# Expert items of 32 rows in four column groups of TensorE, sums kept in four PSUM banks, a ring of ten weight slots, and an opening in halves

## The reference

```python
def first_block(x, attn_norm, w_in, ...):
    for l in range(DEPTH):                      # 2 layers
        h = rms_norm(x, attn_norm[l])
        proj = h @ w_in[l]                      # the first products of the kernel
        ...                                     # retention, sparse attention, gating, FFN
def moe_ffn(h, router_w, router_b, w_gu, b_gu, w_down, b_down):
    logits = (xt @ router_w + router_b).astype(f32)
    top_val, top_idx = lax.top_k(logits, TOP_K) # 4 of 32 experts for each token
    gate = jax.nn.softmax(top_val, axis=-1)
    ...                                         # tokens grouped by expert
    gu = xblk @ w_gu[e] + b_gu[e]               # 1024 -> 2048
    g, up = gu[:, :D_FF_2], gu[:, D_FF_2:]
    g = jnp.minimum(g, SWIGLU_LIMIT)
    up = jnp.clip(up, -SWIGLU_LIMIT, SWIGLU_LIMIT)
    act = (up + 1.0) * (g * jax.nn.sigmoid(SWIGLU_ALPHA * g))
    act @ w_down[e] + b_down[e]                 # 1024 -> 1024, times the gate, summed per token
h = h + g2 * rmsnorm(ff, ffn_post_g)            # ff: the sum over the token's experts
```

## Time and profile before

| | us |
|---|---|
| median of three runs | 1902.48 (1902.21 to 1903.59) |
| the profiled execution | 1903.54 |
| its span, first to last instruction | 1901.6 |
| PE busy | 1843.2 (97%) |
| PE busy in gate-up, L2087 (x2000) | 440.0 |
| PE busy in down, L2110 (x912) | 203.2 |
| DVE busy | 771.0 (41%) |
| DVE L1405, additions to the accumulator (x136) | 93.5 |
| longest wait of SP: for PE L2087, 80 times | 291.2 in total |

### The profile page before, as it was taken

The page is one execution under the profiler, slowest core; times in us unless marked ns, Lnnn a source line. Parts: engine busy times, 40 slices in busy tenths (PEclk is TensorE's granted clock), DMA queues, the critical chain, the costliest instruction groups (busy, mean ns, idle before and its releaser), DMA issues.

```text
span 1901.6 us, 22803 instructions
## 1 busy us (share of the span) xinstructions
PE 1843.2 (97%) x8198; PEld 920.0 (48%) x8199; DVE 771.0 (41%) x1594; ACT 231.2 (12%) x466; POOL 207.5 (11%) x398
## 2 busy tenths in 40 slices
PE   8999999999999999999899999999999999999997
PEld 4466777754667777675433333333333333333332
DVE  3553111135635774288542333233233233323334
ACT  1321000004211000223100100010010001000101
POOL 0200000002004867512000000000000000000000
PEclk9999999999999999999999999999999999999999
DMA  8143344342338884406699999999999499999995
GB/s 317 67 148 126 132 178 165 123 168 89 127 145 342 316 329 172 160 26 242 236 416 429 427 428 429 428 428 429 429 427 427 203 429 429 429 428 428 429 428 231
DMA packets 41016, 558.01 MB, mean 293 GB/s; under 512 B 4567, under 2 KB 5463, under 8 KB 6525
## 3 DMA queue, kind: packets, MB, share of 16 engines
q1 hardware_dynamic: 40380, 556.13, 70.9%
q10 hardware_dynamic: 576, 1.11, 0.2%
HBM read 556.16 MB, written 1.06 MB: 293 GB/s over the span
## 4 chain that ended last, share of the span: by engine, by line
PE 77%; DMA 13%; DVE 8%; issue 1%; ACT 1%; ACTq 0%; DVEq 0%; SPq 0%; POOLq 0%
PE PS L2087 19%; PE PS L1776 16%; DMA mega<-in_exp_w 12%; PE PS L2110 10%; PE PS L1504 8%; PE PS L1795 8%; PE PS L1681 3%; PE PS L1972 1%; PE PS L2069 1%; PE PS L1818 1%; PE PS L2076 1%; PE PS L1812 1%; DVE K L1421 1%; DVE tb L1422 1%; DVE tmp L1418 1%; DVE tb L1419 1%
## 5 line engine op out<-in xcount | busy, mean ns | idle before, releaser
L2087 PE MATMUL PS<-mega,tb 128*64 128x512 f32 x2000 | 440.0, 594 | 6.2 <-POOLq L2234 6.2
L1776 PE MATMUL PS<-hT,mega 128*128 128x256 f32 x1376 | 300.6, 379 | 0.0
L2087 PEld LDWEIGHTS PS<-mega,tb 128*64 128x64 f32 x2000 | 139.8, 137 | 300.5 <-issue 281.8
L1776 PEld LDWEIGHTS PS<-hT,mega 128*128 128x128 f32 x1376 | 261.1, 190 | 43.0 <-issue 8.6
L2110 PE MATMUL PS<-mega,tb 128*64 128x512 f32 x912 | 203.2, 596 | 3.7
L1504 PE MATMUL PS<-mega,hT 128*128 128x512 f32 (+2 forms) x448 | 187.9, 561 | 3.1 <-ACT hT L448 3.1
L1418 DVE TENSOR_SCALAR tmp<-PS 128x512 f32<-128x512 f32 x34 | 23.5, 692 | 368.9 <-PE PS L2087 368.9
L1795 PE MATMUL PS<-mega,late 128*128 128x512 f32 x352 | 154.7, 593 | 0.0
L1109 DVE TENSOR_TENSOR late<-PS,late 128x512 f32<-128x512 f32 x22 | 15.2, 692 | 270.3 <-PE PS L1776 270.3
L2110 PEld LDWEIGHTS PS<-mega,tb 128*64 128x64 f32 x912 | 64.6, 137 | 120.4 <-issue 118.8
L1504 PEld LDWEIGHTS PS<-mega,hT 128*128 128x128 f32 x448 | 81.7, 192 | 72.2 <-issue 60.0
(11 more groups left out here) (459 smaller groups left out, 1687.5 us busy)
## 6 DMA issues: line engine op xcount, KB each, us to landing
mega<-in_exp_w SPq DMA_DIRECT2D x171, 2048.0 KB, 23.4
mega<-in_w_gate_up SPq DMA_DIRECT2D x22, 2048.0 KB, 8.1
late<-in_exp_w SPq DMA_DIRECT2D x21, 2048.0 KB, 25.4
mega<-in_ada_w SPq DMA_DIRECT2D x12, 2048.0 KB, 9.3
mega<-in_w_in_part SPq DMA_DIRECT2D x10, 2048.0 KB, 9.7
mega<-in_w_down SPq DMA_DIRECT2D x10, 2048.0 KB, 7.3
mega<-in_w_out SPq DMA_DIRECT2D x6, 2048.0 KB, 8.4
mega<-in_w_in SPq DMA_DIRECT2D x4, 2048.0 KB, 8.2
```

What stands on the lines that cost most here:

```text
L1776: ins = pe.matmul(PS[:, 4 + 2 * (i % 2) + part, 256 * f:256 * f + 256], wt[:, k, 256 * part + 128 * f:256 * part + 128 * f + 128], hT[:, k ...
L2087: ins = pe.matmul(PS[64 * h:64 * h + 64, b, :], xg[:, o:o + 64], slot_of(r, s)[:, w:w + 512], start=False, stop=k == KC - 1, skip_group_ch ...
```

## The change

It alters five things.

1. An item holds 32 rows. The reference's counts then give 49 items: 17 experts have one, 13 have two (experts 0, 6, 9, 10, 11, 16, 20, 22, 23, 24, 28, 29, 31), two have three (17 and 18). Gate-up has 4 products of 32 rows by 512 columns a step, in four column groups side by side; down has 4 of 32 rows by 256 columns a step. Gate and up of an item now lie side by side in one bank, so all of DVE's and ACT's operations on an item are 256 columns wide and not 512. Transposes are 2 for each of the activations, the scatter weights and the next rows.
2. The scatter adds into four PSUM banks (4 to 7) over all items, 8 products of 32 by 256 an item; the additions in SBUF are gone. The scatter is one piece, after the gather. The down result, the turned scatter weights and the bias get other banks, and the bias product of the next item stands ahead of down.
3. The ring has ten slots (a new tile, `tenth`), and the PE loop is written for five experts in place of three. A load takes the place of the one ten loads earlier; slot 3 of expert 1 is loaded right after expert 0's six.
4. The end: no additions; ACT's squares read PSUM in four operations of 512, DVE multiplies by the gain out of PSUM.
5. The opening: `x` and the first block come in two halves each, the constants' first part (with the gains) on ACT's queue, the big constants table later; TensorE runs products on zeros while it waits, turns the first half of `x`, does four products of the first block, then turns the second half.

```diff
-SLOTS, SLOT_TURNS = 9, 3
+SLOTS, SLOT_TURNS = 10, 5
@@ SP, opening
-            sp.dma_start(ident, a["constants"][:, 0:K_FLIP]).then_inc(g.s_id, 16)
-            sp.dma_start(x[:], a["x"][0].rearrange("(t p) d -> p t d", p=P)).then_inc(g.s_x, 16)
+            sp.dma_start(x[:, 0, :], a["x"][0, 0:P, :]).then_inc(g.s_id, 16)
...
                 if n == 0:
-                    sp.dma_start(K[:, K_FLIP:K_ALL], a["constants"][:, K_FLIP:K_ALL]).then_inc(g.s_k, 16)
+                    sp.dma_start(ring[:, slot, 0:width // 2], src[:, 0:width // 2]).then_inc(g.r_ssm, 16)
+                    sp.dma_start(x[:, 1, :], a["x"][0, P:2 * P, :]).then_inc(g.s_x, 16)
+                    sp.dma_start(ring[:, slot, width // 2:width], src[:, width // 2:width]).then_inc(landed[slot], 16)
+                    continue
@@ SP, experts
+            sp.wait_ge(landed[3], 16 * LOADS_BEFORE[3] + 16)
+            sp.dma_start(slot_of(1, 3), a["exp_w"][1, 3]).then_inc(landed[3], 16)
...
-                for s in range(3 if e == 1 else 0, RING):
-                    last = (s + 3) % RING
-                    sp.wait_ge(freed[last], (before if s < 3 else done) + (USES_BEFORE[last] + 1))
+                for s in range(4 if e == 1 else 0, RING):
+                    last = (s + 2) % RING
+                    sp.wait_ge(freed[last], (before if s < 4 else done) + (USES_BEFORE[last] + 1))
@@ DVE, one item
-                ch.to(v.tensor_scalar(mgs, PS[:, 0, :], SWIGLU_LIMIT, None, ALU.min), g.m_gs, n + 1)
-                ch(v.tensor_scalar(mus, PS[:, 1, :], SWIGLU_LIMIT, -SWIGLU_LIMIT, ALU.min, ALU.max))
+                ch.to(v.tensor_scalar(mgs, PS[:, 0, 0:256], SWIGLU_LIMIT, None, ALU.min), g.m_gs, n + 1)
+                ch(v.tensor_scalar(mus, PS[:, 0, 256:512], SWIGLU_LIMIT, -SWIGLU_LIMIT, ALU.min, ALU.max))
+                expert_row(ch, after, n + 2)
...
-                add_half(ch, 0, 2 * n + 2)
...
+                ch.to(v.tensor_copy(pwT, PS[:, 1, 256:512]), g.m_pwe, n + 2)
+                modulated(ch, n + 2)
                 scatter_rows(ch, after, n + 2)
@@ PE, opening
+            pe.wait_ge(g.s_tab, 2)
+            zero_products(512, 384)
+            pe.wait_ge(g.s_id, 32)
...
+                    pe.wait_ge(g.r_ssm, 16)
+                    pe.wait_ge(g.s_hd, 1)
+                    part(0, range(4))
+                    pe.wait_ge(g.s_x, 16)
+                    turn_x(1, g.s_xt)
...
+                    part(0, range(4, KC)).then_inc(g.s_pj, 1)
...
+                    part(1, range(KC)).then_inc(g.s_pj, 1)
@@ PE, one item
-                        for b in range(2):
-                            for h in range(2):
-                                w = 2048 * kk + 1024 * b + 512 * h
-                                ins = pe.matmul(PS[64 * h:64 * h + 64, b, :], xg[:, o:o + 64], slot_of(r, s)[:, w:w + 512],
-                                                start=False, stop=k == KC - 1, skip_group_check=True)
+                        for j in range(4):
+                            w = 2048 * kk + 512 * j
+                            ins = pe.matmul(PS[32 * j:32 * j + 32, 0, :], xg[:, o:o + ITEM], slot_of(r, s)[:, w:w + 512],
+                                            start=False, stop=k == KC - 1, skip_group_check=True)
                     ins.then_inc(freed[s], 1)
                 gather(n + 2)
...
+                scatter(n + 1)
...
+                bias_rows(n + 2)
                 pe.wait_ge(g.m_ate, n + 1)
+                pe.wait_ge(g.m_pwe, n + 2)
                 for c in range(KC):
...
-                    for h in range(2):
-                        o = 1024 * (c % 4) + 512 * h
-                        ins = pe.matmul(PS[64 * h:64 * h + 64, 2, :], aT[:, P * (c % 4) + 64 * (c // 4):P * (c % 4) + 64 * (c // 4) + 64],
-                                        slot_of(r, s)[:, o:o + 512], start=c == 0, stop=c == KC - 1, skip_group_check=True)
+                    o = P * (c % 2) + ITEM * (c // 2)
+                    for j in range(4):
+                        w = 1024 * (c % 4) + 256 * j
+                        ins = pe.matmul(PS[32 * j:32 * j + 32, 1, 0:256], aT[:, o:o + ITEM], slot_of(r, s)[:, w:w + 256],
+                                        start=c == 0, stop=c == KC - 1, skip_group_check=True)
```

More of the change, by code:

```diff
@@ L333, in slot_of @@
             at = (6 * r + s) % SLOTS
-            return late[:, 0:4096] if at == SLOTS - 1 else mega[:, 4096 * at:4096 * at + 4096]
-        oacc = hTf.rearrange("p (t n) -> p t n", t=TT)
+            if at >= 8:
+                return late[:, 0:4096] if at == 8 else tenth[:]
+            return mega[:, 4096 * at:4096 * at + 4096]
+        normed = hTf.rearrange("p (t n) -> p t n", t=TT)
         tmp2 = tmp[:, 0:1024]
@@ L914, in _ @@
                     link.to(v.tensor_tensor(brow, PS[0:NH, 2, :], oh[0:NH, 512:1024], ALU.add), g.s_b0, 1)
+                else:
+                    v.wait_ge(g.s_par, 16 * l + 16)
+                    for t in range(TT):
+                        v.wait_ge(g.s_xt, TT * l + t + 1)
+                        turned(g.s_hd, TT * l, t, par[:, PC_ATTN:PC_ATTN + 8])
+                        row_squares(t)
                 rsqrt(mean_eps(2, D), 2, dst=y_in)
                 v.sem_inc(g.s_y, 1)
-                if l == 0:
-                    v.wait_ge(g.s_k, 16)
                 projected(0)
@@ L1374, in _ @@
             ends, owner = tmp[:, 0:32], tmp[:, 64:64 + MAX_ITEMS]
-            link(v.tensor_scalar(ends, PS[:, 0, 64:96], 64.5, None, ALU.is_gt))
-            for lim_ in (128.5, 192.5):
-                link(v.scalar_tensor_tensor(ends, PS[:, 0, 64:96], lim_, ends, ALU.is_gt, ALU.add))
+            whole = tmp[:, 128:160].bitcast(I32)
+            link(v.tensor_scalar(ends, PS[:, 0, 64:96], -1.0, 0.0, ALU.add, ALU.max))
+            link(v.tensor_copy(whole, ends))
+            link(v.tensor_scalar(whole, whole, 5, None, ALU.logical_shift_right))
+            link(v.tensor_copy(ends, whole))
             link(v.tensor_tensor_scan(tmp[:, 32:64], K[:, K_ONE:K_ONE + 32], ends, 0.0, ALU.mult, ALU.add))
@@ L2042, in turn_gathered @@
                 pe.wait_ge(g.m_xr, value)
-                for c in range(4):
-                    ins = pe.transpose(PS[:, 3, P * c:P * c + P], xr[:, P * c:P * c + P], ident)
+                for c in range(2):
+                    ins = pe.transpose(PS[:, 3, 256 + P * c:256 + P * c + P], xr[:, P * c:P * c + P], ident)
                 ins.then_inc(g.m_xt, 1)
@@ L2055, in _, with summed @@
             pe.wait_ge(g.act2, ACT2["m_gc"] + 1)
-            for b, bank in enumerate((2, 4, 6, 7)):
-                rows_b = slice(32 * b, 32 * b + 32)
-                ins = pe.matmul(PS[:, bank, :], gT[rows_b, P * (b // 2):P * (b // 2) + P], p2[rows_b, Q_BD + 512 * (b % 2):Q_BD + 512 * (b % 2) + 512],
-                                start=True, stop=True)
+            def summed(t, j):
+                return PS[:, 4 + j, 256 * t:256 * t + 256]
+            for t in range(TT):
+                for j in range(4):
+                    rows = slice(32 * j, 32 * j + 32)
+                    ins = pe.matmul(summed(t, j), gT[rows, P * t:P * t + P], p2[rows, Q_BD + 256 * j:Q_BD + 256 * j + 256],
+                                    start=t == 0, stop=False, skip_group_check=True)
             ins.then_inc(g.pe2, 1)
@@ L2063, in _, with bias_rows @@
             items = pe.value_load(item_i[0:1, ENDS_AT + 31:ENDS_AT + 32], min_val=N_EXPERTS, max_val=MAX_ITEMS)
[L2065 to L2069 removed]
+            def bias_rows(value):
+                pe.wait_ge(g.m_es, value)
+                pe.matmul(PS[:, 0, :], esel, bgu, start=True, stop=False, skip_group_check=True)
+            def scatter(value):
+                pe.wait_ge(g.m_pwe, value)
+                pe.wait_ge(g.m_ye, value)
+                for t in range(TT):
+                    for j in range(4):
+                        rows = slice(32 * j, 32 * j + 32)
+                        ins = pe.matmul(summed(t, j), pwT[rows, P * t:P * t + P], ysb[rows, :], start=False, stop=False, skip_group_check=True)
                 ins.then_inc(g.m_s, 1)
             def item(n, r):
[L2073 to L2076 removed]
                 pe.wait_ge(g.m_xge, n + 1)
@@ L2128, in _ @@
                     item(n, r)
-            pe.wait_ge(g.m_ye, items + 1)
-            pe.wait_ge(g.m_pwe, items + 1)
-            for t in range(TT):
-                for h in range(2):
-                    rows = slice(64 * h, 64 * h + 64)
-                    ins = pe.matmul(PS[:, 3 * t + h, :], pwT[rows, P * t:P * t + P], ysb[rows, :], start=True, stop=True)
-                ins.then_inc(g.m_s, 1)
+            scatter(items + 1)
         @block.gpsimd
```

218 lines of the change are left out of this document (116 added, 102 removed).

## The result

The changed kernel takes 1908.6 us, the median of nine runs (1907.5 to 1910.4), beside 1902.5 for the kernel before on the same chip, also nine runs (1901.7 to 1903.9). The ratio is 1.0032, with a 95% interval of 1.0022 to 1.0042. So it is slower, by 6.1 us, where 4.0 us faster was forecast. Its profiled execution has a span of 1905.9 us, where 1897.6 was worked out.

A forecast was written before the change was run, and what follows sets the result against it. Transfers were to become the bound: last slot at 1872.0, remaining work to 1903.2, less 7.5 for the opening, plus 0.9 and 1.0: span 1897.6, median 1898.5 us. Likeliest case (0.60) 1891 to 1905; with rivals 1885 to 1912.

The forecast's parts named there:

- The item: Expert loop: gate-up 6.84, 3.34 until down, down 3.43 us; 13.6 an item, 13.7 with a gap.
- it just fits: Between gate-up and down: TensorE's own work of 3.4 us fits beside the chain of 3.3.
- P': Time from one item to the next in the changed kernel: 13.7 us, said to count seven times in the end.
- The stream's start: Weight transfers resume at 967.0 on the earlier profile's axis; tenth slot wins 4.9 us, expert 0's second item costs 11.0.
- 182 loads: Weight loads still to go once the stream resumes, at 4.90 us each.
- Experts 17 and 18: Stream stands 1.5 and 11.7 us around these experts of three items, 13.2 in place of 25.4.
- The end: After the last slot at 1872.0: 2.2, 1.7 and a whole item, then a tail of 13.6 us, to 1903.2.
- The opening: Kernel start: first product at 7.4, first block's work done at 34.3, 7.5 us earlier, carried through to the end.
- two additions: Added to 1895.7: 0.9 us for reading the next expert's loop bounds, 1.0 for half clock behind waits.
- Groups that overlap less: Rival, column groups: with three of four overlapping P' is 17.1 and time 1922; today's pairs, over 1965; chance 0.13.
- The clock: Rival: TensorE at half clock in starved items costs 10 us, 1907.5, chance 0.15; its mild form is 1.0 in the sum.
- The stream never stands: Rival: slots come free in time, no stops at the start or experts 17 and 18: 1874, half 1886; chance 0.12.

The follow-up runs named there:

- run 5: Changed kernel with nine slots and three expert bodies in place of ten and five: 1911.6 us, ratio 1.0041 to the kernel before.
- runs 4 to 9: Changed kernel with: one more product an item 1916.2; nine slots, three bodies 1911.6; experts exchanged 0/1 1896.2, 18/26 1895.6, 30/31 1894.9, all three 1870.2 us.
- runs 6, 7 and 9: Changed kernel with experts exchanged in layout: 0 and 1, 1896.2 us; 18 and 26, 1895.6; both pairs and 30 and 31, 1870.2.
- run 2: Kernel before with the new opening, ten slots and five expert bodies, items still of 64 rows: 1893.5 us, ratio 0.9947.
- run 3: Kernel before with the loop over experts written for nine experts in place of three, nothing else: 1913.9 us, ratio 1.0058.

## Why the prediction failed

The mechanism was right: the transfers bind the changed kernel, its faster items win nothing in themselves, and the end follows from start, loads, stops and the items behind the last load. What failed are terms of the sum. They were mis-sized, nearly all to the same side: the item (13.7, measured 14.12), the time until a landing slot can be used (2.2, measured 4.7 at expert 17 and 3.3 at the end), the load (4.90, measured 4.92, 182 times), the change of expert and the opening. Together they are more than the 4.0 us forecast as gain. In the order of the prediction:

- *The item.* Column groups: right. 64 records of 512 columns take 7.05, 64 of 256 take 3.66, four groups side by side at the full rate (6.84 and 3.43 without the last record's tail were forecast). What failed is the step "it just fits". Between gate-up and down TensorE has 3.77 of its own: gather 0.97, scatter 1.08, turned rows and weights 0.77 in all, bias 0.95. I had priced it at 3.4, each piece a little too low, and let DVE's chain of 3.34 set the place. P' is 14.12, not 13.7, and 14.80 across experts, where the gap of 0.66 comes on top; I had allowed 0.45. P' = 14.3 was named as the point where the gain is gone. Its count of seven items is wrong too: in the prediction's own working four of them, and not five, stand round experts 17 and 18 (33.3 to 88.1), so its sum holds six.
- *The stream's start.* Right: first gate-up at 941.03 (941.0 forecast), SP's load for (1,4) at 957.97 (957.7), stream back at 959.4 (959.5).

```profile
941.03 7.07 PE L2141 MATMUL PS<-mega,tb 128*32 128x512 f32 x64 [0.85 <-issue]
```
```profile
957.97 5.48 SPq L432 DMA_DIRECT2D mega<-in_exp_w  x4
```

- *182 loads.* (1873.4 - 959.4 - 17.8)/182 = 4.92 each, 4.90 forecast. 50 more packets of instructions, 0.82 MB or 1.9 us at 428 GB/s, would be nearly half of the 4.4 that this costs.
- *Experts 17 and 18.* 4.1 + 13.7 = 17.8, forecast 1.5 + 11.7 = 13.2. Four items of P' 0.42 too short are 1.7 of the 4.6, the change from 17 to 18 is 0.7. The largest part is the slot's late use. Expert 16's last slot is through at 1412.4 (959.4 and 92 loads), and its products start 4.7 later, where 2.2 was forecast:

```profile
1417.08 1.93 PE L2165 MATMUL PS<-mega,tb 128*32 128x256 f32 x32 [2.35 <-POOLq L2283]
```

  That is 2.5 more; its sixteen parts land over 6.6 us there (run 5). The slower loads take 0.3 of the stop back.
- *The end.* The first item of expert 31 was done 1.4 us later behind the last transfer than forecast. Half clock lengthens it by 2.9, but only 0.3 of that counts: the last slot has landed at 1876.6, 3.2 behind its bytes, and TensorE comes to it at 1877.1 (1875.33 and half of a down). The other 1.1 is again the late use. The second item took 14.1, 0.5 more with rounding. The tail is 12.9, 0.7 less than forecast (17.0 before, from the earlier trace rows; the forecast's own pieces make 13.5, not 13.6).
- *The opening.* 6.5, forecast 7.5: the queries' transposes are at 35.11, where they were at 41.6. The first product starts at 8.44, not 7.4, since the first half of the first block lands late:

```profile
8.44 3.70 PE L1521 MATMUL PS<-mega,hT 128*128 128x512 f32 x8 [1.33 <-DMA mega<-in_w_in_part]
```

  That 1.0 was made good before 941, so the start of the experts doesn't show it. The granted clock is full from 5.9 on, where 7.8 was forecast.

The sum from the forecast's 1895.7 ahead of its two additions: 4.4 for the load rate, 4.6 for the stops, 1.4 for the first item of expert 31, 0.5 for the last item, less 0.7 for the tail: 1905.9, the measured span. The additions (0.9 and 1.0) are within these terms. The stops and the end are taken from this one profile, so that they add up is no second proof; runs 4 to 9 are. Of the 10.2 the long loop has 2.5 and 1.1 by late use and up to 1.9 by its packets, more than the longer items, 2.2.

*The rivals.* Groups that overlap less: out, they overlap fully. The clock: its mild form held. In experts where TensorE waits for each slot the granted clock is low, 0.74 over this stretch:

```profile
1000.00:1020.00 20.00, 11.30 (x80) 0.74 1.01 428
```

  but there TensorE waits for slots anyway; at the start (945 to 960) and in the experts 17 and 18 it is 1.00, and only the last expert pays. The Trainium skill, TensorE: Matmul & The Clock Gate, section Loop structure matters more than you think, says that waits for transfers between products turn the clock down: this trace agrees, and its price here is 0.3 us and not the 10 of that rival. (The row of 943 that the prediction leaned on, bears on it less than said: the waits of TensorE ahead of it, 1.2 and 0.4 us, are for DVE.) The stream never stands: it stood, and runs 6, 7 and 9 show what it would have been worth.

The forecast lay 4 us from no change and hung on an item's length six times and twice on the time until a slot can be used. Its own range for the likeliest case, up to 1905, was too narrow for terms nearly all of which were rounded down.

## What to carry to other kernels

When a faster loop hands the bound to the transfers, work out the end as start of the stream, loads, stops and work behind the last load, and look at which of the loop's turns touch these: here 6 to 9 of 49 items decide, and exchanging three pairs of experts is worth 38 us in a kernel where the halved items by themselves had brought a loss. Count a slot as landed when its last part is there, not when its bytes are through on the mean, and keep a loop's body short where a stream feeds it. Between two products add up TensorE's own small work record by record, tails and all, before letting another engine's chain set the gap. In a ring like this one a slot comes free only with its last use, so uneven work belongs in the middle of the sequence and apart, with light work first and last.

## What the runs showed of the hardware

- A jump back over a long loop body costs TensorE a pause. With three bodies (before, run 5) there are 36 and 38 instruction packets and no such wait; with five of the long bodies 86 packets and pauses of 6.9 to 8.2 us at each of five jumps while the transfers run at 425 to 427 GB/s; with nine short bodies 69 packets and pauses of 5.4 and 3.6. Five short bodies (run 2) don't show it: 38 packets.
- With such a loop the sixteen parts of a load of 2 MiB drift apart, to 6.6 us in the changed kernel and 6.3 in run 3, and come together again when the stream stops for a moment; with a short loop they stay within 2.2 (before, run 5).
- Four products of 32 rows side by side run at a quarter of a full one each in a stream of 64, at 256 and at 512 columns: 3.66 and 7.05 us.
- TensorE with some 2 us of products and 3 of waiting in turn is granted 0.70 to 0.92 of its clock over most such stretches of 20 us (0.74 from 1000 to 1020), but 1.00 from 1580 to 1600, where it is busy 13.3 of 20; in the experts of two items it is back at 1.00.
